# Stage boundaries worked in two token groups, the residual multiplied by a diagonal of inverse norms, and 20 modulation blocks placed in the mLSTM stage

## The reference, cut to what matters

```python
for l in range(2):
    last = l == 1
    mod = (silu(c) @ w_mod[l] + b_mod[l])             # 6 rows of 1024 for the image tokens
    mod_c = silu(c_ctx) @ w_mod[l] + b_mod[l]         # and 6 for the context tokens
    sh1, sc1, ga1, sh2, sc2, ga2 = split(mod, 6)
    h  = rms_norm(x,  g_pre_mix[l]) * (1 + sc1)  + sh1
    hc = rms_norm(xc, g_pre_mix[l]) * (1 + csc1) + csh1
    parts = split(h @ w_in[l]); parts_c = split(hc @ w_in[l])
    # mLSTM, grouped-query attention and windowed attention, merged by gates, then w_out
    x = x + ga1 * rms_norm(o, g_post_mix[l])
    f = conv_ffn(rms_norm(x, g_pre_ffn[l]) * (1 + sc2) + sh2, w_up[l], ..., w_down[l])
    x = x + ga2 * rms_norm(f, g_post_ffn[l])
    # xc in the same way, unless last
return x
```

## Time and profile before

| | |
|---|---|
| median of 3 runs | 1989.17 us (1988.55 to 1992.53) |
| profiled execution | 1991.57 us, its span 1989.8 us |
| busy share of the span | TensorE 92%, weight load 75%, VectorE 65%, ScalarE 43%, GpSimd 30% |
| granted TensorE clock, mean | 0.97 |
| DMA | 249.64 MB, mean 125 GB/s |

### The profile page before, as it was taken

The page is one execution under the profiler, slowest core; times in us unless marked ns, Lnnn a source line. Parts: engine busy times, 40 slices in busy tenths (PEclk is TensorE's granted clock), DMA queues, the critical chain, the costliest instruction groups (busy, mean ns, idle before and its releaser), DMA issues.

```text
span 1989.8 us, 26636 instructions
## 1 busy us (share of the span) xinstructions
PE 1837.7 (92%) x9704; PEld 1496.3 (75%) x9704; DVE 1287.8 (65%) x2199; ACT 862.5 (43%) x1342; POOL 592.5 (30%) x360
## 2 busy tenths in 40 slices
PE   5788979999998999989899999977999999979998
PEld 5777768666786666777788887856768877969997
DVE  6998766532677566794799887346744465557873
ACT  6463544434333443324443442225445345446653
POOL 3244433111111111222232232213313132445564
PEclk9999989999998999999999999988999999989999
DMA  6545533111223222451344447232312233434553
GB/s 251 186 157 180 194 117 102 43 33 54 64 75 132 95 102 74 148 191 58 114 157 148 138 179 245 83 138 90 122 32 96 75 122 102 142 134 148 191 180 129
DMA packets 69383, 249.64 MB, mean 125 GB/s; under 512 B 7696, under 2 KB 9872, under 8 KB 68752
## 3 DMA queue, kind: packets, MB, share of 16 engines
q1 hardware_dynamic: 66096, 241.21, 35.6%
q10 hardware_dynamic: 3168, 6.82, 1.0%
HBM read 246.95 MB, written 1.05 MB: 125 GB/s over the span
## 4 chain that ended last, share of the span: by engine, by line
PE 58%; DVE 27%; ACT 7%; issue 4%; DMA 4%; SPq 0%; ACTq 0%; DVEq 0%
PE bank L530 41%; DVE w_lo L1429 6%; DVE mod_w L1473 4%; PE bank L782 4%; PE bank L759 4%; DVE conv L2197 3%; PE bank L768 2%; DMA w_raw<-in_weights 2%; ACT w_hi L961 2%; DVE probT L1473 2%; PE bank L820 2%; PE bank L879 2%; DMA mod_w<-in_mod_weights 1%; DVE junk_rows L1473 1%; PE bank L868 1%
## 5 line engine op out<-in xcount | busy, mean ns | idle before, releaser
L484 POOL TENSOR_TENSOR w_lo<-w_raw,w_hi 128x512 fp32r<-128x512 f32 x356 | 592.3, 1675 | 1383.0 <-ACT w_hi L961 1365.2
L1429 DVE TENSOR_TENSOR w_lo<-w_raw,w_hi 128x512 fp32r<-128x512 f32 x356 | 363.0, 1035 | 343.0 <-ACT w_hi L961 342.2
L961 ACT ACTIVATE w_hi<-w_raw 128x1024 fp32r<-128x1024 f32 x356 | 367.9, 1053 | 421.1 <-PE bank L530 276.2
L530 PE MATMUL bank<-hT_hi,w_hi 128*128 128x512 f32 (+1 forms) x1344 | 472.0, 351 | 6.7 <-DVE w_lo L1429 5.3
L530 PE MATMUL bank<-hT_hi,w_lo 128*128 128x512 f32 (+1 forms) x1344 | 459.2, 342 | 0.0
L530 PE MATMUL bank<-hT_lo,w_hi 128*128 128x512 f32 (+1 forms) x1344 | 459.2, 342 | 0.0
L530 PEld LDWEIGHTS bank<-hT_hi,w_hi 128*128 128x128 f32 x1344 | 255.0, 190 | 49.5 <-issue 17.3
L530 PEld LDWEIGHTS bank<-hT_hi,w_lo 128*128 128x128 f32 x1344 | 255.0, 190 | 29.3
L530 PEld LDWEIGHTS bank<-hT_lo,w_hi 128*128 128x128 f32 x1344 | 255.2, 190 | 28.3 <-issue 1.4
L1473 DVE SCALAR_TENSOR_TENSOR mod_w<-mod_w,c_rows 128x1024 f32<-128x1024 f32 x96 | 136.4, 1421 | 7.8 <-DMA mod_w<-in_mod_weights 7.5
L530 PE MATMUL bank<-w_hi,hT_hi 128*128 128x512 f32 x320 | 134.1, 419 | 7.6 <-DVE hT_lo L2173 6.8
(11 more groups left out here) (318 smaller groups left out, 3009.0 us busy)
## 6 DMA issues: line engine op xcount, KB each, us to landing
w_raw<-in_weights SPq DMA_DIRECT2D x356, 512.0 KB, 4.1
mod_w<-in_mod_weights SPq DMA_DIRECT2D x96, 512.0 KB, 3.6
nbias<-in_window_bias ACTq DMA_DIRECT2D x16, 192.0 KB, 3.2
resid_x<-in_x ACTq DMA_DIRECT2D x2, 512.0 KB, 6.4
c_rows<-in_conditions SPq DMA_DIRECT2D x1, 1024.0 KB, 11.7
gatew<-in_gate_weights SPq DMA_DIRECT2D x1, 1024.0 KB, 7.9
decay<-in_decay SPq DMA_DIRECT2D x1, 1024.0 KB, 5.8
resid_c<-in_ctx ACTq DMA_DIRECT2D x1, 1024.0 KB, 5.7
```

The costliest lines, as they stand in the source:

```text
L484: nc.gpsimd.tensor_tensor(w_lo[:, s, 0, :], w_raw[:, s, 0:COLS], w_hi[:, s, 0, :].bitcast(F32), ALU.subtract).then_inc(lo0_ready, 1)
L530: mm = pe.matmul(held[key][:, oc], st, mv_, start=(opens and k == 0 and t == 0 and i == 0), stop=(closes and k == tiles - 1 and t == 2), s ...
L961: a.activation(w_hi[:, p % RING].rearrange("p k n -> p (k n)"), w_raw[:, p % RING, :], ACT.Copy).then_inc(hi_ready, 1)
L1429: v.tensor_tensor(w_lo[:, p % RING, 1, :], w_raw[:, p % RING, COLS:KP * COLS], w_hi[:, p % RING, 1, :].bitcast(F32), ALU.subtract).then_in ...
```

## The change

**Normalisation by a product.** VectorE no longer writes `xn`. It writes `diag`, the 128x128 identity times the inverse norms of a tile (`norm_diag`), and TensorE multiplies the residual by it in float32, which transposes and normalises in one (`norm_T`). A bank now holds two blocks k of one token group.

**Token groups.** The tokens of a boundary are taken in two groups, tiles 0 and 1, then tiles 2 and 3; in layer 1's ffn tile 2, then tile 3 (`groups`). The first product of the next stage (`gemm_by_groups`) runs pieces 0 and 1 for group 0, then `norm_T` of group 1, then pieces 2 and 3 for group 0, and then all four pieces for group 1. The four pieces stay in the ring until group 1 has passed. `norm_T` of group 0 comes right behind the last product of the stage before; in the first boundary it stands between c = 0 and c = 1 of `out`. VectorE and ScalarE work on group 0 (`norm_tmp`, `norm_hi`, `norm_lo`) while they still finish the last tile's residual, with splits of weight pieces between.

**Modulation.** The last 20 blocks are loaded and used in layer 1's mLSTM stage, no longer in layer 0's `w_down` stage.

**Layout and buffers.** `hT_hi` and `hT_lo` are stored by half of the tokens, so a product over all 512 tokens reads two segments of 256. `onrm`, `o_ffn`, the junk outputs of the squares and a second `ptmp` lie elsewhere.

The core of the diff:

```diff
-    at += [FIRST_DOWN + 4 + 4 * k // 5 for k in range(20)]
+    at += [FIRST_ML + 1 + p for p in (2, 3, 3, 4, 5, 6, 6, 7, 8, 8, 9, 9, 10, 10, 11, 11, 12, 12, 13, 13)]
...
-    hT_hi = sb("hT_hi", [P, KD, TT], 16 * KB, F32R)
+    hT_hi = sb("hT_hi", [P, 2, KD, T], 16 * KB, F32R)
...
+    def groups(l, which):
+        return [[2], [3]] if l == LAYERS - 1 and which == "ffn" else [[0, 1], [2, 3]]
...
+            def norm_T(l, which, gi, pool="rot"):
+                of = groups(l, which)[gi]
+                for t in of:
+                    pe.wait_ge(*diag_ready.at((l, which, t)))
+                for p in range(KD // 2):
+                    ps = take(pe, ("nT", l, which, gi, p), pool)
+                    for j in range(2):
+                        k = 2 * p + j
+                        for n, t in enumerate(of):
+                            o = (j * len(of) + n) * P
+                            mm = pe.matmul(ps[:, o:o + P], resid[t // 2][:, t % 2, k * P:(k + 1) * P], diag[:, t, :],
+                                           start=True, stop=True)
...
+            def gemm_by_groups(banks, l, which):
+                for gi, of in enumerate(groups(l, which)):
+                    a, b = of[0] * P, (of[-1] + 1) * P
+                    for p in range(n):
+                        if gi == 0 and p == n // 2:
+                            norm_T(l, which, 1)
+                        pe.wait_ge(*hT_ready.at((l, which, gi, p)))
+                        for key, pool_, subs, stationary in banks:
...
             for c in range(2):
+                if c == 1:
+                    norm_T(0, "mix", 0, "ret")
                 gemm_tok(("out", c), [0, 1], mix_hi, mix_lo, tiles=4, opens=False, closes=False,
...
-                norm_T(l, "ffn", q_tts)
-                for c in range(FB // 2):
-                    gemm_T(("up", l, c), qs, hT_hi, hT_lo, inputs=None if c else normed(l, "ffn"))
+                norm_T(l, "ffn", 0)
+                up = blocks_T(("up", l, 0), 4, None, qs)
+                gemm_by_groups([(key, "acc" if g < 2 and not last else "rot", subs, True) for g, (key, subs) in enumerate(up)], l, "ffn")
+                for c in range(1, FB // 2):
+                    gemm_T(("up", l, c), qs, hT_hi, hT_lo)
...
+            def norm_diag(l, which, t):
+                dve.wait_ge(*root_ready.at((l, which, t)))
+                v.reciprocal(ss[:, 4 + t:5 + t], rs[:, 56 + t:57 + t]).then_inc(*W.next())
+                dve.wait_ge(*W.last())
+                v.tensor_scalar(diag[:, t, :], ident, ss[:, 4 + t:5 + t], None, ALU.mult)\
+                    .then_inc(*W.tell(diag_ready, (l, which, t)))
...
             for p in range(KD // 2):
+                norm_tmp(0, "mix", 0, p)
+                norm_lo(0, "mix", 0, p)
+                split_lo(LAST_OUT + 1 + p)
...
-                if l == 0 and which == "ffn":
-                    for k in range(10):
-                        mod_ops(1)
-                        split_lo(FIRST_DOWN + 15 + 4 * k // 5)
-                    mod_bias(1, 24, MOD_BLOCKS, 1, 96)
...
                     if h < MH:
                         ml_weights(h)
+                        mod_ops(2 * spare)
+                if last:
+                    mod_bias(1, 24, MOD_BLOCKS, 1, 96)
```

More of the change, by code:

```diff
@@ L691, in _ @@
             out_last()
-            def norm_T(l, which, tts):
-                for t in tts:
-                    pe.wait_ge(*xn_ready.at((l, which, t)))
-                for k in range(KD):
-                    ps = take(pe, ("nT", l, which, k))
-                    for t in tts:
-                        mm = pe.transpose(ps[:, t * P:(t + 1) * P], xn[:, t, k * P:(k + 1) * P], ident)
-                    mm.then_inc(*filled(("nT", l, which, k)))
-            def normed(l, which):
-                return lambda p: hT_ready.at((l, which, KP * p + KP - 1))
             def spread(l, which, sets):
@@ L1101, in _, with norm_root, norm_hi @@
                     .then_inc(*A.tell(root_ready, (0, "mix", t)))
+            def norm_root(l, which, t, junk):
+                act.wait_ge(*resid_ready.at((l, which, t)))
+                a.activation(junk, resid[t // 2][:, t % 2, :], ACT.Square, accum_out=ss[:, 56 + t:57 + t]).then_inc(*A.next())
+                act.wait_ge(*A.last())
+                a.activation(rs[:, 56 + t:57 + t], ss[:, 56 + t:57 + t], ACT.Sqrt, scale=1.0 / D, bias=eps[:])\
+                    .then_inc(*A.tell(root_ready, (l, which, t)))
+            def norm_hi(l, which, gi, p):
+                act.wait_ge(*hT_tmp_ready.at((l, which, gi, p)))
+                a.activation(normed_pair(hT_hi, l, which, gi, p), ntmp_pair(l, which, gi, p), ACT.Copy)\
+                    .then_inc(*A.tell(hT_hi_ready, (l, which, gi, p)))
+            for p in range(KD // 2):
+                norm_hi(0, "mix", 0, p)
+                split_hi(LAST_OUT + 1 + p)
             for t in range(NT):
@@ L1108, in _, with output @@
                     .then_inc(*A.tell(root_ready, ("b1out", t)))
-            def norm_root(l, which, t):
-                act.wait_ge(*resid_ready.at((l, which, t)))
-                a.activation(xn[:, t, :], resid[t // 2][:, t % 2, :], ACT.Square, accum_out=ss[:, 56 + t:57 + t]).then_inc(*A.next())
-                act.wait_ge(*A.last())
-                a.activation(rs[:, 56 + t:57 + t], ss[:, 56 + t:57 + t], ACT.Sqrt, scale=1.0 / D, bias=eps[:])\
-                    .then_inc(*A.tell(root_ready, (l, which, t)))
-            def norm(l, which, tts):
-                t0 = tts[0] * P
-                for k in range(KD):
-                    ahead(("nT", l, which, k))
-                    act.wait_ge(*hT_tmp_ready.at((l, which, k)))
-                    a.activation(hT_hi[:, k, t0:TT], ptmp[:, k % 4, t0:TT], ACT.Copy).then_inc(*A.tell(hT_hi_ready, (l, which, k)))
-            def output(l, which, w, tts, o, junk, gains, nxt):
+                norm_root(0, "mix", 2 + t, sg[:, t, :])
+            split_hi(LAST_OUT + 8)
+            for p in range(KD // 2):
+                norm_hi(0, "mix", 1, p)
+            def output(l, which, w, tts, gains, nxt):
                 for c in range(2):
@@ L1132, in output @@
                         key = ((w, l, c), g)
-                        ahead(key)
+                        final = c == 1 and nxt is not None and g == len(tts) - 1
+                        o, junk = o_of(which, t), junk_of(which, t)
+                        if final:
+                            after = piece("w_up", l, 0) if which == "mix" else piece("w_in_2", l + 1, 0)
+                            split_hi(after + 2)
+                        else:
+                            ahead(key)
                         act.wait_ge(*filled_at(key))
@@ L1171, in _ @@
                 lag, conv_cols = ffn_lag(l)
-                if l == 0:
-                    for t in range(2, 4):
-                        norm_root(0, "mix", t)
-                norm(l, "mix", tts)
                 def slots(keys, evacuate, tiles=KD, beside=None):
@@ L1414, in _ @@
                             .then_inc(*A.tell(fT_hi_ready, (l, done)))
-                output(l, "ffn", "down", q_tts, o_ffn, junk_ffn, gain_ffn, None if last else (l + 1, "mix"))
+                output(l, "ffn", "down", q_tts, gain_ffn, None if last else (l + 1, "mix"))
             act.wait_ge(out_stored, 32)
@@ L1752, in norm @@
+            norm_gains(0, "mix")
+            for t in range(NT):
+                norm_diag(0, "mix", t)
+            for p in range(KD // 2):
+                norm_tmp(0, "mix", 0, p)
+                norm_lo(0, "mix", 0, p)
+                split_lo(LAST_OUT + 1 + p)
+            for t in range(NT):
+                for c in range(2):
+                    key = (("out", c), t)
                     ahead(key)
                     dve.wait_ge(*filled_at(key))
-                    if k >= 4:
-                        dve.wait_ge(*hT_hi_ready.at((l, which, k - 4)))
@@ L2209, in _ @@
                 if not last:
-                    for k in range(10):
-                        mod_ops(1)
-                        if k in (3, 6, 9):
-                            split_lo(FIRST_DOWN + 5 + k // 3)
                     mod_bias(1, 0, BOTH_MODS, 2, 64)
                     mod_bias(1, BOTH_MODS, 24, 1, 72)
-                post(l, "ffn", "down", q_tts, o_ffn, gain_ffn, None if last else (l + 1, "mix"))
+                post(l, "ffn", "down", q_tts, gain_ffn, None if last else (l + 1, "mix"))
     es.close()
```

250 lines of the change are left out of this document (157 added, 93 removed).

## The result

The changed kernel takes 1998.07 us (median of 20 runs, 1993.41 to 2003.49), the kernel before 1991.3 (20 runs, 1987.29 to 1995.28). The ratio is 1.0035, 95% interval [1.0026, 1.0044]: slower by 7 us, where 23 us faster was forecast. The profiled execution took 1997.64 us, its span grew from 1989.8 to 1995.9.

A forecast was written before the change was run, and what follows sets the result against it. TensorE was taken to bound the kernel, working in nearly all of the 1989.8 us span, so its gaps could be won. Terms -23.6 + 3.4 - 3.5 - 5.5 + 0.0 + 6.3 gave -22.9 us: 1966, range 1956 to 1989.

The forecast's parts named there:

- Term 2: Layer 1's mLSTM stage: the 20 modulation blocks moved there cost +3.4 us, bounds +0.5 and +8, most products finding VectorE idle.
- the circle: Layer 0's w_down: weight load, split, dot product and block load wait on each other, one to two blocks a turn.
- rival D: mLSTM stage: SyncE again holds weight loads behind blocks, costing 36 us instead of 3.4; time 1998.9, chance 0.09.
- Term 1: Layer 0's w_down: without modulation blocks the two chunks get back 5.7 and 17.9 us, together -23.6.
- Term 4: Boundary to layer 0's ffn: token groups gain 3.5 us, bounds 0 and -7.
- Terms 5: Boundary to layer 1's mix: token groups gain 5.5 us, bounds -9 and -1.
- Term 6: Boundary to layer 0's mix: out_last ends some 8 us later, norm_T of group 1 about 10 behind; net 0.0, -3 to +6.
- Term 7: Boundary to layer 1's ffn: one-tile groups make 192 matmuls of 128 columns at 0.122 us, cost +6.3.
- rivals B: Layer 1's ffn: fp32r at 128 columns runs at float32's rate, 0.241; +27.7 us there, time 1987.7, chance 0.14.
- C: Layer 1's ffn: 128 columns cost half of 256, 0.061; -2.2 us there, time 1957.8, chance 0.10.
- Term 3: Normalising product at boundaries: 0.241 us each against near 0.16 per transpose, +2.6 us per boundary, counted inside the boundary schedules.
- Rival E: The boundaries give nothing, as the last tile's chain lengthens by all it gained; sum -7.9, time 1981.3, chance 0.09.

## Why the prediction was wrong

**Term 2, where it failed.** The step reads "Most find VectorE idle. Two places are not covered", sum +3.4. It priced the products by VectorE's time only and took SyncE's queue for free. Measured: 21.9. VectorE's part is 5.3 to 5.8 (6.1 without token groups), near the forecast and inside its bound of 8; the queue's is 16.1 to 16.6. I had described the circle for the down stage from the earlier trace rows and had written it down as rival D, with a chance of 0.09. Its mechanism was right, and so was its sign: the waits for `w_raw` in the mLSTM stage are tens of us, 50.1. Its price (36) was too high. What fits is that one turn of the circle now carries up to two blocks: ScalarE waited 10 times there, for 20 blocks, against 8 times in the second down chunk for 10. That D's time, 1998.9, is within 1 us of the measured one is luck: it has 14 us too much for the stage and none of the 9.7 of the bank waits.

The error behind it is the sentence against D: "VectorE's idle share there, and products that don't each follow the split of the newest piece". An idle share says nothing of a circle, since the circle is itself made of waiting. And the condition I gave, that VectorE is late by more than four pieces' time, is not the one that counts. SyncE's queue can't be four pieces ahead if it has to stop at a block whose buffer VectorE frees only after splitting the pieces up to there. The order of the code shows this: a lead of 0 to 2 in the new place, as bad as in the old one. The order was at hand, and the two counts would have put D first.

**Term 1** held: -23.5 for -23.6, the first chunk to 60.6 us and the second to 59.9 against the 60 to 61 named. But its explanation, that the blocks must leave, was too strong; later loads do as much for the second chunk. In the first chunk, where the leads were 3 or 4 for most blocks, moving the blocks did win 5.6 us. TensorE has one long wait there in the kernel before, for a split that stands on VectorE behind two dot products:

```profile
1211.12 2.32 DVE L1473 SCALAR_TENSOR_TENSOR mod_w<-mod_w,c_rows 128x1024 f32<-128x1024 f32 x1
...
1213.57 2.10 DVE L1473 SCALAR_TENSOR_TENSOR mod_w<-mod_w,c_rows 128x1024 f32<-128x1024 f32 x1
...
1215.59 1.74 DVE L1429 TENSOR_TENSOR w_lo<-w_raw,w_hi 128x512 fp32r<-128x512 f32 x1
```

```profile
1217.59 0.73 PE L530 MATMUL bank<-w_hi,fT_hi 128*128 128x512 f32 x1 [3.67 <-DVE w_lo L1429]
```

So most of that part seems to belong to VectorE's work and not to the lead. That is argued from these rows and the leads; no run took it apart.

**Term 4** held for the boundary (T + 32.9 for T + 33.8) and in its steps: the second `norm_T` starts at T + 11.8 (954.73), where 12.2 was forecast, and in layer 1's mix at T + 11.8 too. But it stopped there. The next chunk's bank was not looked at, and 8.0 us went there. "Where a stall goes, what is late next" was answered only up to the end of the first chunk. In the kernel before, eight banks of transposes and four of `up` go through the rotation of six, and the second chunk gets a bank free by then. The change put two of the chunk's four banks into another pool and four transposing banks between, and the rotation came round to a bank still in use.

**Terms 5, 6 and 7** held within 1.1 us: -6.6 for -5.5, -0.4 for 0.0, +6.9 for +6.3. Term 6 held in its steps as well: `out_last` ended at 273.7, 8.4 us later (8 forecast), and the second `norm_T` began 10.8 behind it (10 forecast). Term 7's number is partly luck. 0.111 us for a matmul of 128 columns was near the 0.122 taken; rivals B (0.241) and C (0.061) fell. The Trainium skill ("TensorE: Matmul & The Clock Gate", "Back-to-back issue gap") gives about 81 ns for it; the runs here show 111, so for these fp32r matmuls the measurement decides against it. The gain in price, 192 x 0.011 = 2.1 us, was lost to the clock, half of full for 10 us (about 4.7 us), which the term did not have.

**Term 3.** 32 records of `norm_T` (16 products) took 3.73 to 3.81 us, 0.23 to 0.24 a product, as `spread` had shown. But its price for a transpose, 0.16, mixed two levels of the clock. The transposes followed the long idle times, and in each boundary the first of them ran at half of the full clock. Two stretches of the transposes of layer 1's mix in the kernel before, and a `norm_T` of the changed kernel at the full clock:

```profile
1355.00:1357.00 2.00, 2.00 (x11) 0.50 0.00 0
1357.50:1359.00 1.50, 1.50 (x15) 0.98 0.00 0
```

```profile
942.89 3.73 PE L652 MATMUL bank<-diag,resid_c 128*128 128x128 f32 x32
```

One transpose begins every 0.21 us at half clock and every 0.11 at full. At the full clock the product costs 0.23 against 0.11, a factor of 2.1 and not 1.5. The factor of four between transposing and multiplying that the Trainium skill states in the table of terms of "TensorE: Matmul & The Clock Gate" does not show here either. The terms held all the same, because they took only the product's price, and in the changed kernel the `norm_T` of the first three boundaries ran at the full clock.

**Rival E** fell: three boundaries gained 11.4 us together and lost 8.0 to the bank. The two segments that a product of 512 columns reads cost nothing that shows: between the splits of pieces 156 and 188 the changed kernel needs 174.9 us for eight chunks, and so does the kernel before with late loads in the down stage (the kernel before itself 176.0).

**The account.** Of the 29 us between forecast (-22.9) and span (+6.1), 18.5 are the mLSTM stage, 9.7 the two bank waits; the rest cancels to about 1.

## What to carry to other kernels

Where one queue loads for two users, look, for each wait in it, how far ahead of its user the next load of the other kind is at the moment when the wait ends. That number comes from the order of the instructions alone. Here it decided whether the queue loaded ahead: with a lead of 0 to 2 ScalarE waited 47 to 50 us, with 3 almost nothing. Moving the blocks to an idler stage with the same small lead moved the loss along. A loss that vanished from one stage after a move is to be looked for where the work went, before anything else is tuned.

Splitting a stage in two groups paid here where the pieces stayed 256 columns wide, and not at 128, where the matmul count doubled and the price hardly fell. It also changes the rotation of banks behind it: follow the rotation one chunk further than the change.

## What the runs showed of the hardware that was not expected

The granted clock fell to 0.50 (1.2 GHz) from 1782.5 to 1792.5 us though TensorE had stood idle only 0.56 and 1.95 us in the 6 us ahead, and it was busy all through that stretch with matmuls of 128 columns. In the kernel before, the clock fell at the same boundary inside the idle time of 10.86 us, about 2 us after its start (TensorE by stretch):

```profile
1778.80:1780.60 1.80, 0.02 (x1) 1.00 0.01 5
1780.70:1789.60 8.90, 0.00 (x0) 0.51 0.54 177
```

There the half clock fell mostly on idle time, where it cost nothing; with the two groups it fell on 10 us of matmuls. So avoiding the long idle time did not avoid the slow stretch. Which of the two short waits or the narrow matmuls brought it on was not tried. At the boundaries to layer 0's ffn and layer 1's mix, with waits of 0.39 to 1.80 us and matmuls of 256 columns, the granted clock stayed at 1.00.
